# Order of the products within a form: 512 columns first, then 256

## The reference

```
def swiglu(h, wg, wu, wd):
    return (jax.nn.silu(h @ wg) * (h @ wu)) @ wd
...
h = rms_norm(x, ffn_norm[layer, 0])
x = x + 0.5 * swiglu(h, ffn_w_gate[layer, 0], ffn_w_up[layer, 0], ffn_w_down[layer, 0])
```

## Time and profile before

| | before |
|---|---|
| median of 3 runs | 1682.64 us (1681.64 to 1683.5) |
| profiled execution | 1682.69 us, span 1680.9 us |
| TensorE busy | 1663.0 us, 99% of the span, 8628 products |
| TensorE weight loads busy | 1382.7 us, 82%, 8628 loads |
| VectorE busy | 1333.2 us, 79% |
| ScalarE busy | 857.8 us, 51% |
| GpSimd busy | 235.0 us, 14% |
| line 981, 512 columns | 1152 + 864 products |
| line 983, 256 columns | 1152 + 864 products |

### The profile page before, as it was taken

One profiled execution on the slowest core, in us unless ns is written; L12 is line 12 of the kernel. 1 busy time (PEld: TensorE's weight loads), 2 busy tenths in 40 slices (PEclk: granted clock), 3 DMA queues, 4 the chain that ended last, 5 costly groups with the idle time before them and its releaser, 6 DMA issues.

```text
span 1680.9 us, 22465 instructions
## 1 busy us (share of the span) xinstructions
PE 1663.0 (99%) x8628; PEld 1382.7 (82%) x8628; DVE 1333.2 (79%) x1626; ACT 857.8 (51%) x1072; POOL 235.0 (14%) x243
## 2 busy tenths in 40 slices
PE   8999999999999999999999999999999999999999
PEld 6888888887876688888888888888888878888887
DVE  6988888867778658888888788888887798888885
ACT  7455456353237545545545455545454654554551
POOL 0151111032014220111110201111111001111100
PEclk9999999999999999999999999999999999999999
DMA  8576876362420034686774446776851357768741
GB/s 220 138 181 147 198 165 153 98 149 71 103 67 26 14 100 138 159 204 141 177 184 101 126 125 156 178 182 149 195 131 63 102 135 178 178 148 198 165 115 61
DMA packets 275377, 231.95 MB, mean 138 GB/s; under 512 B 19748, under 2 KB 234760, under 8 KB 275272
## 3 DMA queue, kind: packets, MB, share of 16 engines
q1 hardware_dynamic: 255992, 162.80, 34.4%
q0 software_dynamic: 18432, 67.12, 21.4%
q10 hardware_dynamic: 848, 0.61, 0.2%
HBM read 160.89 MB, written 2.10 MB: 97 GB/s over the span
## 4 chain that ended last, share of the span: by engine, by line
PE 88%; DVE 8%; ACT 2%; issue 2%; DMA 0%; ACTq 0%; DVEq 0%
PE ps_s L981 27%; PE ps_s L983 13%; PE ps_y L797 6%; PE ps_y L799 6%; PE ps_y L798 6%; PE ps_s L797 4%; PE ps_s L799 4%; PE ps_s L798 4%; PE ps_aux L799 2%; PE ps_aux L797 2%; PE ps_aux L798 2%; PE ps_stat L799 2%; PE ps_stat L798 2%; PE ps_stat L797 2%; PE ps_s L1205 1%
## 5 line engine op out<-in xcount | busy, mean ns | idle before, releaser
L981 PE MATMUL ps_s<-xt,w_hi 128*128 128x512 f32 x1152 | 410.9, 399 | 4.1 <-ACT out_rows L1385 2.6
L983 PE MATMUL ps_s<-xt,w_lo 128*128 128x256 f32 x1152 | 323.4, 281 | 0.0
L1887 DVE TENSOR_TENSOR w_lo<-raw,w_hi 128x1024 fp32r<-128x1024 f32 (+2 forms) x210 | 252.9, 1207 | 84.7 <-ACT w_hi L1385 81.9
L1385 ACT CAST w_hi<-raw 128x1024 fp32r<-128x1024 f32 (+1 forms) x212 | 217.6, 1029 | 179.5 <-PE ps_s L983 111.1
L981 PE MATMUL ps_s<-xg,w_hi 128*128 128x512 f32 x864 | 308.2, 398 | 0.0
L981 PEld LDWEIGHTS ps_s<-xt,w_hi 128*128 128x128 f32 x1152 | 216.4, 188 | 60.1 <-ACT out_rows L1385 3.7
L983 PE MATMUL ps_s<-xg,w_lo 128*128 128x256 f32 x864 | 242.6, 281 | 0.0
L983 PEld LDWEIGHTS ps_s<-xt,w_lo 128*128 128x128 f32 x1152 | 217.6, 189 | 0.0
L1385 ACT CAST w_hi<-raw_b 128x1024 fp32r<-128x1024 f32 (+2 forms) x138 | 140.6, 1019 | 117.8 <-PE ps_s L983 62.0
L1887 DVE TENSOR_TENSOR w_lo<-raw_b,w_hi 128x1024 fp32r<-128x1024 f32 (+2 forms) x138 | 165.1, 1197 | 37.9 <-ACT w_hi L1385 35.6
L981 PEld LDWEIGHTS ps_s<-xg,w_hi 128*128 128x128 f32 x864 | 162.3, 188 | 39.8
(11 more groups left out here) (394 smaller groups left out, 3011.5 us busy)
## 6 DMA issues: line engine op xcount, KB each, us to landing
scratch<-in_ffn_w_down SPq DMA_DIRECT2D x64, 512.0 KB, 7.8
raw<-raw POOLq DMA_DIRECT2D x64, 512.0 KB, 6.0
raw_b<-in_ffn_w_gate SPq DMA_DIRECT2D x80, 256.0 KB, 6.4
raw_b<-in_ffn_w_up SPq DMA_DIRECT2D x80, 256.0 KB, 6.0
raw<-in_ffn_w_gate SPq DMA_DIRECT2D x64, 256.0 KB, 6.4
raw<-in_ffn_w_up SPq DMA_DIRECT2D x64, 256.0 KB, 5.7
raw_b<-raw_b POOLq DMA_DIRECT2D x32, 512.0 KB, 5.6
raw<-in_hyb_w_in SPq DMA_DIRECT2D x18, 512.0 KB, 3.9
```

The lines of the kernel that those rows point to most:

```text
L981: mm(bank, weight(w_hi, n, at, at + P), x_both, start=m in (0, 1, 3) and k == 0, stop=False, skip_group_check=True)
L983: last_mm = mm(bank[:, H:T], weight(w_lo, n, at, at + P), x_both[:, 0:H], start=False, stop=k == 3, skip_group_check=True)
L1385: return nc.scalar.copy(dst, src)
L1887: tt(shaped(weight(w_lo, n, 0, BLOCKS[n] * P)), source, shaped(f32(weight(w_hi, n, 0, BLOCKS[n] * P))), ALU.subtract).then_inc(lo_ready, 1)
```

## The change

Within a form, the loop over (j, k) is written as a list. The eight products of 512 columns with w_hi come first, for both banks; then the eight of 256 columns with w_lo, in the same order of (j, k). The wait ahead of the form is now for the high parts of its unit, and the wait for the low parts stands between the two groups. Operands, flags and the semaphore at the end of the form are as they were. The new function `x_of(k)` gives the moving operand that `x_both` was.

```diff
--- before.py
+++ after.py
@@ -970,18 +970,21 @@
                     pe.wait_ge(added, 3 * q + 2)
                 if s == FIRST and m == 2:
                     pe.wait_ge(xt_lo_ready, 2 * ffn + 2)
+                parts = [(form_banks(m)[:, j, :], k, (4 * j + k) * P) for j in range(2) for k in range(4)]
+
+                def x_of(k):
+                    x_at = 2 * T * (k + 4 * (m > 0)) + (0 if m == 5 else T)
+                    t_at = ({2: 1, 4: 2, 6: 3}.get(m, 0) * 4 + k) * T
+                    return xg[:, x_at:x_at + T] if m in (0, 1, 5) else xt[:, t_at:t_at + T]
+
+                pe.wait_ge(hi_ready, n + 1)
+                for bank, k, at in parts:
+                    mm(bank, weight(w_hi, n, at, at + P), x_of(k), start=m in (0, 1, 3) and k == 0, stop=False,
+                       skip_group_check=True)
                 pe.wait_ge(lo_ready, n + 1)
-                for j in range(2):
-                    bank = form_banks(m)[:, j, :]
-                    for k in range(4):
-                        x_at = 2 * T * (k + 4 * (m > 0)) + (0 if m == 5 else T)
-                        t_at = ({2: 1, 4: 2, 6: 3}.get(m, 0) * 4 + k) * T
-                        x_both = xg[:, x_at:x_at + T] if m in (0, 1, 5) else xt[:, t_at:t_at + T]
-                        at = (4 * j + k) * P
-                        mm(bank, weight(w_hi, n, at, at + P), x_both, start=m in (0, 1, 3) and k == 0, stop=False,
-                           skip_group_check=True)
-                        last_mm = mm(bank[:, H:T], weight(w_lo, n, at, at + P), x_both[:, 0:H], start=False, stop=k == 3,
-                                     skip_group_check=True)
+                for bank, k, at in parts:
+                    last_mm = mm(bank[:, H:T], weight(w_lo, n, at, at + P), x_of(k)[:, 0:H], start=False, stop=k == 3,
+                                 skip_group_check=True)
                 last_mm.then_inc(unit_done, 1)
 
             def half_round(ffn, h):
```

## The result

The changed kernel takes 1673.94 us (median of 5 runs, 1673.73 to 1674.32) against 1682.54 for the kernel before (1681.64 to 1683.5). The ratio is 0.9949, 95% interval 0.9936 to 0.9961: 8.6 us less. The forecast was 1674.1, the range 1669.0 to 1680.5.

What follows compares the result with a forecast made beforehand. It took TensorE's own rate as the bound. 36 steps of 0.25 us gave 9.0, less 0.3 at waits and 0.1 in one stage, so 1682.7 - 8.6 = 1674.1 us (67%); range 1669.0 to 1680.5.

Steps and rivals of the forecast that it cites:

- The bound: Whole kernel: TensorE's own rate, the distance between product starts, limits it; low parts come early, 0.65 us ahead at the tightest.
- The products: In the forms: 2.795 us each, 2.771 for a step's first; seven take 19.54 against 19.77, 0.23 saved.
- The products behind: Half round (only 512s) after a step's seven forms: loses 0.03 us before settling instead of 0.05, so 0.02 saved.
- The added wait: One more wait per form, 252 in all: costs between 0 and 12.9 us, taken as 0 because TensorE's sequencer runs ahead.
- The sum: Whole kernel: 36 steps of 0.25 us give 9.0, less 0.3 at waits and 0.1 in one stage: 8.6 saved.
- Never settling: Rival, 17%: in the forms, 512s lose 0.05 us after every change of width; 2.9 less 0.4 saved, 1680.2 us.
- Settled throughout: Rival, 8%: in the forms, 512s lose nothing after eight 256s; 15.1 less 0.4 us saved, 1668.0 us.
- No change: Rival, 4%: product order within forms doesn't matter and low parts were never late; 1682.7 us.
- Slower by uncovered loads: Rival, 4%: in rows of 256s, weight loads stick out from under short products; 122 us lost less 9 gained, about 1796.

Runs made afterwards that it cites:

- Experiments 1: Changed kernel with the wait for low parts back at the form's head and none in the middle: 1674.88 us, ratio 0.9955 to the kernel before.
- experiment 2: Kernel before, old alternating order, with only the waits moved: high parts at the form's head, low parts behind the first 512-column product; 1682.49 us against 1682.51.
- experiment 9: Kernel before, old alternating order, only the weight loads of high parts (under the 256-column products) halved to 64 columns: 1659.03 us, ratio 0.9861.
- experiment 5: Changed kernel with groups of two 512s and two 256s, low-part wait at the form's head: 1672.55 us, ratio 0.9943 to the kernel before.

## Why the prediction was right

*The bound.* Right: TensorE's own rate, no wait for low parts. Experiments 1 and 2 show it from both sides, each moving the one and not the other.

*The products.* Right to within 0.02 us a step: 2.795 for a form against 2.79 measured, 2.771 for the first against 2.76, 19.54 for seven against 19.52. That both transitions stood in the trace of before, with the same loads, carried it.

*The products behind.* 0.02 forecast, 0.03 measured (2.55 to 2.52).

*The added wait.* Taken at 0 between 0 and 12.9 us, and it was 0: experiment 2, with the wait and no gain to hide it, gives 1682.49 against 1682.51. The reason given isn't shown. The prediction had 252 more sequencer instructions of 51 ns, hidden because the sequencer is ahead of the array; there are none more to hide, since the wait stands on a weight load that was there before.

*The sum.* 8.6 forecast and 8.6 measured, but that they meet to a tenth is luck, since two terms were off against each other. A step gained 0.25 + 0.03 = 0.28, not 0.25, so 36 steps 10.1 us; and what is lost again was 0.4 in the forecast, while the span fell by only 1680.9 - 1672.1 = 8.8, so 1.3 were lost. Five of the 36 steps, those in which TensorE waits for results of ScalarE and VectorE, account for 0.9 of it: from step start to half round the five gained 0.44 us together where five others gain 1.22, and the half rounds behind them 0.03 where 0.18 is usual. One of them, in the kernel before and in the changed kernel:

```profile
1008.22 0.39 PE L981 MATMUL ps_s<-xg,w_hi 128*128 128x512 f32 x1
...
1028.15 0.39 PE L797 MATMUL ps_y<-turn_hi,w_hi 128*128 128x512 f32 x1
```

```profile
1003.83 1.98 PE L982 MATMUL ps_s<-xg,w_hi 128*128 128x512 f32 x8
...
1023.80 0.40 PE L797 MATMUL ps_y<-turn_hi,w_hi 128*128 128x512 f32 x1
```

It took 1028.15 - 1008.22 = 19.93 us and now takes 1023.80 - 1003.83 = 19.97. The forecast let each wait eat the 0.03 of one form; in fact the form with the step's first wait got 0.04 to 0.09 longer, which takes back from half to more than all of what the forms ahead of it in the step had gained. The step shown also held the three forms that ran at 2.78 before. The other 0.4 lies behind the last step of each of the four parts. No half round stands there, so the forecast counted 36 where there are 32, and the stretches from there to the next part's first form, or the program's end, grew by 0.26 us together, for which no row here gives a cause.

*The rivals.* Never settling: the half round's products are at 0.227 after six. Settled throughout: the 0.03 after 256s is there in every form that follows another. No change: the order moved 8.6 us. Slower by uncovered loads: the 256s hold 0.119. Its mechanism had something in it all the same. Halving the load under a 256 wins most in the old order (experiment 9), so what I took for a price of changing width may in part be that; it is argued, not shown, since the same order with whole loads can also run at 0.347 a pair. The prediction didn't need the cause, since it took its durations from rows in which the new order already stood; experiment 5, where I worked with the supposed cause, went wrong by 6 to 10 us.

## What to carry to other kernels

On a kernel bound by TensorE, read the distance from start to start for each pair of neighbours, not the records' durations: here the same products cost 2.82 or 2.79 us by their order alone. Where a profile already holds the order that is planned (a run of one width, the change to another), take the sum from there, and try small groups too, since twos beat fours here for no reason that the count of changes gives. Turning every other group, so that equal widths meet at the border, won 1.9 us more.

## What the runs showed of the hardware

Products of 512 and 256 columns with whole loads of 128 columns settle at 0.227 and 0.120 us; alternating they take 0.353 a pair, and by groups of one, two, four and eight a form takes 2.82, 2.787, 2.81 and 2.79 us, not in the order of the groups' size. With loads of 64 columns the alternating pair takes 0.340, less than the two settled places with whole loads together (0.347). The pace isn't fixed by the order alone: behind some waits the alternating order with whole loads went over to 0.347 a pair, 2.78 a form, for the rest of the step. Why the patterns repeat as they do, and which waits change them, stays open.
